# A decoder layer on one core: the last residual by identity matmuls for ten of sixteen tiles, Ln and Exp from one table set, and a later wait for the reloaded residual

## The reference, cut to what matters

```python
def _rmsnorm(x, g):
    xf = x.astype(jnp.float32)
    y = xf * lax.rsqrt(jnp.mean(xf * xf, axis=-1, keepdims=True) + RMS_EPS)
    return (y * g.astype(jnp.float32)).astype(x.dtype)

def _layer(x, ...):
    h = _rmsnorm(x, g_mix_pre)
    q, k, v, iq, ik, iw, u = jnp.split(h @ w_in, ...)
    a = attn_fn(q, k, v, iq, ik, iw)          # top-k sparse attention
    p, new_pool = _pool_mixer(u, pool_buf, pos0, pool_w, pool_scale)
    x = x + _rmsnorm(concat([a, p]) @ w_o, g_mix_post)
    f, new_conv = _conv_ffn(_rmsnorm(x, g_ffn_pre), conv_buf, w_up, conv_w, conv_b, w_down)
    return x + _rmsnorm(f, g_ffn_post)
```

## Time and profile before

| | |
|---|---|
| median of 3 runs | 1199.91 us (1198.22 to 1200.7) |
| the profiled execution: time, span | 1201.06 us, 1199.2 us |
| mean granted TensorE clock | 0.981 |
| busy: PE, DVE, ACT, POOL | 1152.5, 812.9, 536.3, 64.9 us |
| chain that ended last: PE, DVE, DMA | 87%, 4%, 3% |

### The profile page before, as it was taken

How to read it: one execution, slowest core, us unless ns; L and a number is a source line. 1 busy time by engine, 2 the same in 40 slices (tenths; PEclk the granted TensorE clock), 3 DMA queues, 4 the chain that set the end, 5 groups by cost and what they waited for, 6 DMA issues and landing times.

```text
span 1199.2 us, 25793 instructions
## 1 busy us (share of the span) xinstructions
PE 1152.5 (96%) x9130; PEld 1114.8 (93%) x9130; DVE 812.9 (68%) x1524; ACT 536.3 (45%) x750; POOL 64.9 (5%) x70
## 2 busy tenths in 40 slices
PE   8999999999998999999999999999998999999992
PEld 8879999768996999999999999999998999999992
DVE  4776798776478877777777777777775444444444
ACT  7343333333346654545454545454544333443331
POOL 4710000000003100000000000000000000000002
PEclk9999999999999999999999999999999999999996
DMA  8888779768852655555555555555556666666641
GB/s 307 305 273 270 252 240 305 232 211 287 307 170 76 213 178 189 167 185 171 184 167 189 165 188 170 179 174 176 178 172 202 196 184 181 176 177 179 184 133 72
DMA packets 81079, 238.75 MB, mean 199 GB/s; under 512 B 9440, under 2 KB 28992, under 8 KB 78704
## 3 DMA queue, kind: packets, MB, share of 16 engines
q1 hardware_dynamic: 75152, 225.40, 58.5%
q10 hardware_dynamic: 4480, 9.01, 2.2%
q0 software_dynamic: 1408, 3.84, 1.0%
HBM read 231.64 MB, written 24.16 MB: 213 GB/s over the span
## 4 chain that ended last, share of the span: by engine, by line
PE 87%; DVE 4%; DMA 3%; SPq 2%; issue 1%; ACT 1%; DVEq 0%; POOL 0%; ACTq 0%; POOLq 0%
PE bank L1465 28%; PE bank L1466 28%; PE bank L1468 28%; DMA raw<-in_w_in 1%; DVE part L1337 1%; DMA x<-xscr 1%; DVE lo L440 1%; DMA cache_ring<-kscr 1%; SPq L482 1%; SPq L483 1%; PE bank L1658 1%; PE bank L1682 1%; SPq L481 1%; DVE h_lo L1342 0%; DVE o L1444 0%
## 5 line engine op out<-in xcount | busy, mean ns | idle before, releaser
L1465 PE MATMUL bank<-h_hi,hi 128*128 128x266 f32 (+1 forms) x2096 | 603.6, 288 | 1.0 <-DVE lo L440 1.0
L1468 PE MATMUL bank<-h_hi,lo 128*128 128x266 f32 (+1 forms) x2096 | 602.5, 287 | 0.0
L1466 PE MATMUL bank<-h_lo,hi 128*128 128x266 f32 (+1 forms) x2096 | 601.6, 287 | 0.0
L440 DVE TENSOR_TENSOR lo<-raw,hi 128x1024 fp32r<-128x1024 f32 (+2 forms) x362 | 431.5, 1198 | 214.1 <-ACT hi L432 190.5
L432 ACT ACTIVATE hi<-raw 128x1024 fp32r<-128x1024 f32 (+2 forms) x362 | 373.5, 1034 | 293.8 <-PE bank L1468 263.2
L1465 PEld LDWEIGHTS bank<-h_hi,hi 128*128 128x128 f32 x2096 | 397.0, 189 | 5.5 <-issue 3.7
L1466 PEld LDWEIGHTS bank<-h_lo,hi 128*128 128x128 f32 x2096 | 395.6, 189 | 0.1
L1468 PEld LDWEIGHTS bank<-h_hi,lo 128*128 128x128 f32 x2096 | 395.3, 189 | 0.0
L1465 PE MATMUL bank<-g_hi,hi 128*128 128x264 f32 x704 | 200.9, 285 | 5.3 <-DVE lo L440 5.3
L1466 PE MATMUL bank<-g_lo,hi 128*128 128x264 f32 x704 | 201.7, 286 | 0.0
L1468 PE MATMUL bank<-g_hi,lo 128*128 128x264 f32 x704 | 200.8, 285 | 0.0
(11 more groups left out here) (273 smaller groups left out, 634.4 us busy)
## 6 DMA issues: line engine op xcount, KB each, us to landing
raw<-in_w_up SPq DMA_DIRECT2D x176, 512.0 KB, 4.2
raw<-in_w_in SPq DMA_DIRECT2D x56, 512.0 KB, 5.5
raw<-in_w_down SPq DMA_DIRECT2D x64, 448.0 KB, 3.5
raw<-in_w_o SPq DMA_DIRECT2D x32, 512.0 KB, 4.4
raw<-in_w_down SPq DMA_DIRECT2D x32, 512.0 KB, 3.7
kscr<-in_cache_k SPq DMA_DIRECT2D x64, 128.0 KB
vscr<-in_cache_v SPq DMA_DIRECT2D x64, 128.0 KB
mixed<-kscr SPq DMA_DIRECT2D x8, 512.0 KB, 7.1
```

What stands on the lines that cost most here:

```text
L440: ops.tensor_tensor(lo[:, s, 0:width], raw[:, s, 0:width], hi[:, s, 0:width].bitcast(F32), ALU.subtract).then_inc(done, 1)
L1465: mm(out, w_hi, x_hi[:, k, first:], start=(opens and done == 0), stop=False)
L1466: mm(out, w_hi, x_lo[:, k, first:], start=False, stop=False)
L1468: last = mm(out, w_lo, x_hi[:, k, first:], start=False, stop=(closes and done == total))
```

## The change

Four edits, all in how work is placed and ordered.

1. The last residual. Of the sixteen tiles the first ten (`Y_SUMS`: two, two, three and three) are summed in PSUM: PE puts `x2` into a bank by a matmul with the identity (`residual_in`), DVE only multiplies `o2` by `rms`, PE adds that product by a second matmul with the identity, and ACT copies the sum to `o2`. Seven banks take turns (`SUM_BANKS`). Tiles 10 to 15 stay on DVE, in two groups of three, and GpSimd has none. SP stores the six groups in the order of tiles.
2. The sum of squares of the last tile. ACT squares the sixteenth tile straight when its matmuls are done, and DVE moves the tile out after that. PE takes the sum of the first fifteen from `sumsq` and adds the sixteenth square from `sq` by a second matmul into `misc`.
3. The table set. `natural_log_exp_and_others` is loaded by name at the start and after the last gate.
4. DVE waits for `x2_loaded` only before it scales the tiles whose residual it adds itself; PE waits for it ahead of its first `residual_in`. Apart from these, each sample's attention values have a semaphore of their own in place of one for two samples.

```diff
-Y_PARTS = [(0, 2), (2, 5), (5, 8), (8, 11)]
-Y_POOL = [(11, 13), (13, 16)]
+Y_SUMS = [(0, 2), (2, 4), (4, 7), (7, 10)]
+Y_PARTS = [(10, 13), (13, 16)]
+SUM_BANKS = [2, 3, 4, 5, 6, 0, 1]
+ROOT_TABLES = "natural_log_exp_and_others"
...
-    v_loaded = [sem(f"v_loaded{j}") for j in range(GROUPS)]
+    v_loaded = [sem(f"v_loaded{b}") for b in range(DB)]
...
# SyncE
+            for k0, k1 in Y_SUMS:
+                sp.wait_ge(y_act, k1)
                 sp.dma_start(a["y"][:, k0:k1, :], o2[:, k0:k1, :]).then_inc(stored, 16)
+            for n, (k0, k1) in enumerate(Y_PARTS):
+                sp.wait_ge(y_ready, n + 1)
+                sp.dma_start(a["y"][:, k0:k1, :], o2[:, k0:k1, :]).then_inc(stored, 16)
# GpSimd
-            pool.wait_ge(rms_ready, 4)
-            for n, (k0, k1) in enumerate(Y_POOL):
-                scale_rms(nc.gpsimd, k0, k1).then_inc(o_scaled_pool, 1)
-            for n, (k0, k1) in enumerate(Y_POOL):
-                pool.wait_ge(o_scaled_pool, n + 1)
-                nc.gpsimd.tensor_tensor(o2[:, k0:k1, :], x2[:, k0:k1, :], o2[:, k0:k1, :], ALU.add).then_inc(y_pool, 1)
# ScalarE
             ae.dma_start(par[:, 0:CWT], a["par"][:, 0:CWT]).then_inc(par_loaded, 16)
+            nc.scalar.preload_act_table_set(ROOT_TABLES)
...
             gated_hi(FT - 1)
+            nc.scalar.preload_act_table_set(ROOT_TABLES)
             ae.wait_ge(chunk_used, C_DOWN)
             ae.dma_start(x2[:, :, :], xscr).then_inc(x2_loaded, 16)
...
-                ae.wait_ge(o_ready, KM + n + 1)
+                if tail and t == 1:
+                    ae.wait_ge(chunk_used, 4 * r + C_DOWN + 6 * (t + 1))
+                else:
+                    ae.wait_ge(o_ready, KM + n + 1)
...
             root(4, N_META)
+            for k in range(Y_SUMS[-1][1]):
+                ae.wait_ge(y_sum_done, k + 1)
+                nc.scalar.activation(o2[:, k, :], bank[SUM_BANKS[k % 7]][:, 0:TG], ACT.Copy).then_inc(y_act, 1)
# VectorE
-            dve.wait_ge(x2_loaded, 16)
-
             def down_out(i, t, r, tail=False):
...
                 dve.wait_ge(chunk_used, 4 * r + C_DOWN + 6 * (t + 1))
+                if tail and t == 1:
+                    dve.wait_ge(sq_ready, 4 * KM)
                 nc.vector.tensor_scalar(o2[:, bass.ds(n, 1), :], ...).then_inc(o_ready, 1)
-                dve.wait_ge(sq_ready, 3 * KM + n + 1)
-                nc.vector.tensor_tensor(sumsq[:, N_META:], ...).then_inc(sq_used, 1)
-                dve.wait_ge(sq_used, 3 * KM + n)
+                if not (tail and t == 1):
+                    ... (the same three lines)
...
+            dve.wait_ge(o_ready, 2 * KM)
             inv_rms(4, N_META)
+            for k0, k1 in Y_SUMS:
+                scale_rms(nc.vector, k0, k1).then_inc(y_prod_ready, 1)
+            dve.wait_ge(x2_loaded, 16)
+            for k0, k1 in Y_PARTS:
+                scale_rms(nc.vector, k0, k1).then_inc(o_scaled_dve, 1)
+            for n, (k0, k1) in enumerate(Y_PARTS):
+                dve.wait_ge(o_scaled_dve, n + 1)
+                nc.vector.tensor_tensor(o2[:, k0:k1, :], x2[:, k0:k1, :], o2[:, k0:k1, :],
+                                        ALU.add).then_inc(y_ready, 1)
# TensorE
-            total(4, 4 * KM - 1, N_META)
+            pe.wait_ge(sq_used, 4 * KM - 2)
+            mm(misc[:, N_META:T], con[:, ONE:ONE + P], sumsq[:, N_META:], start=True, stop=False)
+            def residual_in(k):
+                mm(bank[SUM_BANKS[k % 7]][:, 0:TG], ident, x2[:, k, :], start=True, stop=False)
+            pe.wait_ge(x2_loaded, 16)
+            residual_in(0)
+            pe.wait_ge(sq_ready, 4 * KM)
+            mm(misc[:, N_META:T], con[:, ONE:ONE + P], sq[:, 1, N_META:], start=False, stop=True).then_inc(sum_ready, 1)
+            for k in range(1, 5):
+                residual_in(k)
+            pe.wait_ge(o_ready, 2 * KM)
+            residual_in(5)
+            residual_in(6)
+            for n, (k0, k1) in enumerate(Y_SUMS):
+                pe.wait_ge(y_prod_ready, n + 1)
+                for k in range(k0, k1):
+                    if k >= 7:
+                        pe.wait_ge(y_act, k - 6)
+                        residual_in(k)
+                    mm(bank[SUM_BANKS[k % 7]][:, 0:TG], ident, o2[:, k, :], start=False, stop=True).then_inc(y_sum_done, 1)
```

More of the change, by code:

```diff
@@ L399, in build_program @@
     xt_ready = sem("xt_ready")
-    y_pool = sem("y_pool")
-    o_scaled_pool = sem("o_scaled_pool")
+    y_prod_ready = sem("y_prod_ready")
+    y_sum_done = sem("y_sum_done")
+    y_act = sem("y_act")
     o_scaled_dve = sem("o_scaled_dve")
@@ L531, in load_v @@
                     sp.wait_ge(spv_done, 1)
-                sp.dma_start(value_slot(b), kv_src[1][b]).then_inc(v_loaded[b % GROUPS], 16)
+                sp.dma_start(value_slot(b), kv_src[1][b]).then_inc(v_loaded[b], 16)
             def load_wo(n):
@@ L594, in _ @@
                 load_down(i, 1)
-            for done, n, (k0, k1) in ((y_ready, 1, Y_PARTS[0]), (y_ready, 2, Y_PARTS[1]), (y_pool, 1, Y_POOL[0]),
-                                      (y_ready, 3, Y_PARTS[2]), (y_ready, 4, Y_PARTS[3]), (y_pool, 2, Y_POOL[1])):
-                sp.wait_ge(done, n)
+            for k0, k1 in Y_SUMS:
+                sp.wait_ge(y_act, k1)
                 sp.dma_start(a["y"][:, k0:k1, :], o2[:, k0:k1, :]).then_inc(stored, 16)
-            sp.wait_ge(stored, 16 * (4 + len(Y_PARTS) + len(Y_POOL)))
+            for n, (k0, k1) in enumerate(Y_PARTS):
+                sp.wait_ge(y_ready, n + 1)
+                sp.dma_start(a["y"][:, k0:k1, :], o2[:, k0:k1, :]).then_inc(stored, 16)
+            sp.wait_ge(stored, 16 * (4 + len(Y_PARTS) + len(Y_SUMS)))
             sp.wait_ge(u_stored, 16)
@@ L1424, in down_out @@
                 dve.wait_ge(chunk_used, 4 * r + C_DOWN + 6 * (t + 1))
+                if tail and t == 1:
+                    dve.wait_ge(sq_ready, 4 * KM)
                 nc.vector.tensor_scalar(o2[:, bass.ds(n, 1), :], bank[(T_DOWN + t) % 2][:, N_META:T].unsqueeze(1),
                                         par[:, bass.ds(G4 + n, 1)], None, mul).then_inc(o_ready, 1)
-                dve.wait_ge(sq_ready, 3 * KM + n + 1)
-                nc.vector.tensor_tensor(sumsq[:, N_META:], sumsq[:, N_META:], sq[:, t, N_META:], ALU.add).then_inc(sq_used, 1)
-                dve.wait_ge(sq_used, 3 * KM + n)
+                if not (tail and t == 1):
+                    dve.wait_ge(sq_ready, 3 * KM + n + 1)
+                    nc.vector.tensor_tensor(sumsq[:, N_META:], sumsq[:, N_META:], sq[:, t, N_META:],
+                                            ALU.add).then_inc(sq_used, 1)
+                    dve.wait_ge(sq_used, 3 * KM + n)
             with dve.Fori(0, KM // 2 - 1) as i:
@@ L1678, in sample_values @@
                 for j in range(GROUPS):
-                    pe.wait_ge(v_loaded[j], 16 * (r + 1))
+                    pe.wait_ge(v_loaded[GROUPS * r + j], 16)
                 for n in range(PAGES):
@@ L1810, in _ @@
                 down_tile(3 * i, i, 1)
-            total(4, 4 * KM - 1, N_META)
+            pe.wait_ge(sq_used, 4 * KM - 2)
+            mm(misc[:, N_META:T], con[:, ONE:ONE + P], sumsq[:, N_META:], start=True, stop=False)
+            ident = con[:, IDN:IDN + P]
+            def residual_in(k):
[16 more added lines that the diff above has]
+                    mm(bank[SUM_BANKS[k % 7]][:, 0:TG], ident, o2[:, k, :], start=False, stop=True).then_inc(y_sum_done, 1)
     ctx.close()
```

## The result

The changed kernel takes 1185.86 us (median of 4 runs, 1183.83 to 1186.94) against 1199.72 us: ratio 0.9884, 95% interval [0.9866, 0.9901]. That is 13.9 us less; 15.5 less and 1184.4 us had been forecast. The profiled execution took 1183.83 us with a span of 1182.0, for which 1185.6 and 1183.7 had been forecast.

The account below looks back on a forecast made before the run. PE was 87% of the chain, so gains lay where PE idles or another engine carries the end. 8.2 + 1.3 + 6.0 = 15.5 us gave median 1184.4 us; own range 1183 to 1187, full 1181.8 to 1190.6.

Parts of the forecast that it names:

- The wait for x2: At the x2 reload in w_down: PE's 5.50 us standing and 2.7 us from the lower clock both go, 8.2 us.
- The room for the chunk loads: After the reload: chunk 8's load may land 11.9 us after issue; loads there take 3.3 to 5.0 us.
- The table set: At the norms' roots: the exposed load before Exp goes, 1.3 us at the second norm; the fourth's counts in the end.
- the third norm: Before w_up: removing the table load gains nothing, since PE is busy and does not wait until the reload; bounds 0 to 1.3.
- First norm: DVE would be ready 1.3 us earlier but waits 2.10 us for PE's queue, so removing the load gains nothing.
- The rival that adds these roots: First and third norms: both pass their 1.3 us on, giving a median of 1181.9 us; chance 0.07.
- The end: From the last tile's square to the last store: earlier norm, new residual and stores end at 1193.2 against 1199.2, 6.0 us.
- the first rival: At the end: PE's clock falls despite the f32 matmuls, the end gives 0.4 us, median 1190.0; chance 0.14.
- One of the two reasons: Against the lower clock at the end: with PE 3.26 busy of 4.00 in the second norm's stage, the clock stayed 1.00.
- The slower side: At the reload: loads 8 to 11 starve beside x2 and PE stands; landing at 948 would give 1203 us; chance 0.02.
- The semaphores of the values: At the attention values: the same transfers are waited for in the same order, so the change gains nothing.
- The sum: Whole kernel: 15.5 us less, profiled execution 1185.6 us with span 1183.7, median 1184.4; chance 0.62.

Follow-up runs that it names:

- e2: The kernel before with only DVE's wait for x2_loaded moved behind the fourth norm; median 1193.80 us, ratio 0.9947 to the kernel before.
- e1: The changed kernel with DVE's wait for x2_loaded put back ahead of the down tiles; median 1192.13 us, ratio 0.9929 to the kernel before.
- e3: The changed kernel without the two table loads by name, so the compiler places ten loads again; median 1188.61 us, ratio 0.9912 to the kernel before.
- e6: The changed kernel with each residual's identity matmul right ahead of its product's, none during the norm; median 1189.60 us, ratio 0.9910 to the kernel before.
- e5: The changed kernel with all sixteen last-residual tiles on DVE, none on GpSimd or PE; median 1185.74 us, ratio 0.9882 to the kernel before.
- e7: The changed kernel with SP storing DVE's two groups before PE's last one; median 1184.00 us, ratio 0.9869 to the kernel before.

## Why the prediction was right, point by point

*The wait for x2, 8.2 us.* Shown: 8.2 when it is the only edit (e2), 7.6 when it is put back (e1), 5.5 of standing each time and 2.1 to 2.7 of clock. In the change itself the stage to the fourth Ln is 9.1 shorter, of which the earlier sum is 0.9 (from the square or move at the last matmul's end to Ln: 2.23 us before, 1.34 now), so 8.2 again. The room for the chunk loads was enough, with less to spare than I had put: I took 5.0 us as the longest landing, it was 8.0, of 11.9.

*The table set, 1.3 at the second norm.* The length to the reload is 1.2 shorter than before, and 1.6 longer in e3 against the changed kernel. Against the mean of the seven kernels that are alike there (545.4) it is 1.0 and 1.4. That fits 1.3, within the 0.8 by which this length scatters, and leaves next to nothing for the third norm, which lies in the same length. First norm: it lies in the scatter of the first stage and isn't settled; e3 has the shortest first stage of all with its ten loads, which speaks against a gain. The rival that adds these roots has no support.

*The end, 6.0 us.* Measured 5.3 from Ln plus 0.9 before it, 6.2. Ln came 1.34 after the last tile's matmuls where I had 1.6; from Ln to the end I had 14.5, it was 14.56, with PE's thirteen matmuls in 5.9 where I had 5.7, DVE done 0.55 us before the last copy, and the end 4.9 us behind that copy.

*The clock at the end* stayed at 1.00, and e6 shows that this hung on the early residuals, which was the open point behind the first rival. The rival's size, 5.6 us for a clock that is down for the whole stretch, was not reached even without them: it was down for 3.4 us. One of the two reasons that I gave against that rival was weaker than I made it. In the second norm's stage the clock was at 1.00 in the window from 388, but earlier in the same stage, after PE had stood still, it was not:

```profile
374.00:376.00 2.00, 0.00 (x0) 0.00 (x0) 1.71 (x3) 0.91 (x3) 1.86 (x3) 1.00 0.02 4
378.00:380.00 2.00, 2.00 (x8) 1.43 (x7) 2.00 (x4) 1.40 (x3) 1.25 (x3) 0.52 0.03 8
```

These windows of the kernel before look like those of e6: PE idle, PE back at work, and only then the lower clock. The other reason, that matmuls fill the gap, is the one that held.

*The slower side* has no sign: loads are slower, but PE has no wait. The working had twice 3.7 us for a load beside the reload; the longest took 8.0 here and 8.7 in e3. That the reload would itself land later than after 11 us was wrong, it landed after 10.6: beside each other the loads became longer and the reload didn't.

*The sum.* By stage the profiles give 1.2 + 9.1 + 5.3 = 15.6 us against 15.5 forecast. The remaining 1.6 us of the span's difference is the first stage, which differs as much between executions of equal instructions, and in which these two profiles also differ in their time at the lower clock (10.3 against 17.0 us). That the profiled execution came out 1.8 us under its forecast is therefore luck. The median's 13.9 lies 1.7 short of the sum by stage. If one takes the three later lengths and the 1.8 to 1.9 us outside the span off each median, 370.1 us are left for the changed kernel's first stage and 368.3 to 369.6 for the six other kernels with the same one; with their mean, 368.9, the changed kernel would have a median of 1184.6. So I put the shortfall down to scatter, with four runs each. It is the likely account, not a shown one, since only one execution of each kernel has its lengths on record. The semaphores of the values, which lie in the first stage, were not tried by themselves; the six kernels have that edit too.

*Not foreseen* in the working was how the end's gain divides. I had counted GpSimd's absence and the identity matmuls as one; e5 shows that the first alone is 3.45 of 4.0. The order of the stores was foreseen as a cost (1.0 us for a third store behind the last copy), but not that it could be had back: e7 gets 1.35.

## What to carry to other kernels

Put a wait in front of the first instruction that uses the data, not at the border of a stage: an in-order engine that others depend on turns one early wait into a standing PE, and PE pays again at a lower clock when it returns. Before handing work from DVE to another engine, try plain DVE with GpSimd silent; here 32 tile steps alone were faster than 22 beside GpSimd. A much larger edit with 20 matmuls and ten copies gained only another half microsecond, and 1.9 once its stores were in the order in which the data is ready. Read the order of stores at the end against the order in which their data is ready.

## What I had not expected of the hardware

A 792-wide f32 tensor_tensor on DVE takes 0.93 to 0.98 us alone and up to 2.62 beside GpSimd's tensor_tensor, so GpSimd's help cost more than it gave: DVE's 22 tile steps took 12.2 us beside it and 6.7 alone, 5.5 less, while all 32 took DVE 9.7, so the ten others only 3.0 more. After PE stopped, the lower clock came late enough to hit it on its return: in e6 about 1.1 us after PE was at work again (a mean of 0.64 in the window from 1174, so the fall is at 1174.3). The same stall at the reload cost 2.1 us of clock in e1 and 2.7 in the kernel before, although the clock was down for 6.8 us in both: it fell earlier against PE's return in e1, so that more of the low stretch passed while PE still stood.
